# The 16 by 16 diagonal blocks of a delta rule's triangular system, inverted by column elimination on VectorE after a trip through HBM, in place of repeated squaring on TensorE

## The reference, cut to what matters

```
a_kk = where(ii > jj, (kb @ k^T) * decay, 0)     # strictly lower triangular, 64 x 64
m    = a_kk + eye(64)
sol  = triangular_solve(m, [v * beta, kb * exp(gc)], lower, unit diagonal)
```

## Time and profile before

| | |
|---|---|
| median of three runs | 1122.15 us |
| span of the profiled execution, first to last instruction | 1117.9 us |
| the profiled execution's own time | not recorded beside its span; the runs' median lies 4.25 us above this span |
| PE busy | 1053.7 us, 94% |
| DVE, ACT, POOL busy | 279.4, 172.6, 8.5 us |
| read from HBM | 424.29 MB, 382 GB/s over the span |

### The profile page before, as it was taken

How to read it: one execution, slowest core, us unless ns; L and a number is a source line. 1 busy time by engine, 2 the same in 40 slices (tenths; PEclk the granted TensorE clock), 3 DMA queues, 4 the chain that set the end, 5 groups by cost and what they waited for, 6 DMA issues and landing times.

```text
span 1117.9 us, 12901 instructions
## 1 busy us (share of the span) xinstructions
PE 1053.7 (94%) x5140; PEld 448.4 (40%) x5140; DVE 279.4 (25%) x640; ACT 172.6 (15%) x285; POOL 8.5 (1%) x29
## 2 busy tenths in 40 slices
PE   9999999999999999999999888898999898889987
PEld 7866676544343434443333222323333232222322
DVE  3643454432222223331211111111111111111111
ACT  3522344300000000000100000000000000000001
POOL 1000000000000000000000000000000000000000
PEclk9999999999999999999999999999999999999999
DMA  9594137799999999999999999999999999999996
GB/s 325 110 349 180 76 116 293 306 428 399 422 412 425 430 429 429 427 429 430 433 434 429 430 429 431 431 431 429 432 430 428 427 431 433 431 433 424 425 428 281
DMA packets 37931, 427.48 MB, mean 382 GB/s; under 512 B 6243, under 2 KB 8388, under 8 KB 17924
## 3 DMA queue, kind: packets, MB, share of 16 engines
q1 hardware_dynamic: 36628, 426.37, 91.6%
q10 hardware_dynamic: 1264, 0.56, 0.2%
HBM read 424.29 MB, written 2.62 MB: 382 GB/s over the span
## 4 chain that ended last, share of the span: by engine, by line
PE 56%; DMA 37%; DVE 4%; issue 1%; ACT 1%; SPq 0%; DVEq 0%; ACTq 0%
DMA store<-in_w_gate_up_dram 21%; PE bank L1900 18%; DMA store<-in_w_down_dram 15%; PE bank L1950 14%; PE bank L1475 5%; PE bank L1485 4%; PE bank L1676 4%; PE bank L1818 3%; PE bank L1550 2%; PE bank L1880 1%; DVE flow L1329 1%; DMA store<-in_w_in_dram 1%; PE bank L1919 1%; DVE flow L1322 1%; DVE flow L1327 1%
## 5 line engine op out<-in xcount | busy, mean ns | idle before, releaser
L1900 PE MATMUL bank<-store,flow 128*64 128x512 f32 x2048 | 450.9, 596 | 14.0 <-DMA store<-in_w_gate_up_dram 13.1
L1900 PEld LDWEIGHTS bank<-store,flow 128*64 128x64 f32 x2048 | 144.1, 137 | 315.5 <-issue 288.7
L1950 PE MATMUL bank<-store,flow 128*64 128x512 f32 x992 | 230.3, 617 | 33.6 <-DMA store<-in_w_down_dram 21.4
L1322 DVE TENSOR_SCALAR flow<-bank 128x512 f32<-128x512 f32 x32 | 22.1, 692 | 597.4 <-PE bank L1900 597.4
L1950 PEld LDWEIGHTS bank<-store,flow 128*64 128x64 f32 x992 | 74.1, 141 | 169.5 <-issue 143.2
L834 ACT ACTIVATE flow<-flow 128x512 f32<-128x512 f32 x32 | 20.2, 631 | 449.5 <-DVE flow L1322 449.5
L1827 PE MATMUL bank<-qkT 64*128 64x512 f32 x248 | 61.9, 616 | 0.0
L1475 PE MATMUL bank<-store 128*128 128x512 f32 x128 | 57.2, 595 | 0.0
L850 ACT COPY qkT<-bank 128x512 f32<-128x512 f32 x31 | 18.2, 586 | 204.9 <-PE bank L1950 204.9
L1485 PE MATMUL bank<-store 128*128 128x256 f32 x192 | 42.9, 381 | 0.4 <-DMA store<-in_w_in_dram 0.4
L1485 PEld LDWEIGHTS bank<-store 128*128 128x128 f32 x192 | 36.2, 190 | 6.9 <-issue 2.2
(11 more groups left out here) (322 smaller groups left out, 631.4 us busy)
## 6 DMA issues: line engine op xcount, KB each, us to landing
store<-in_w_gate_up_dram SPq DMA_DIRECT2D x38, 4096.0 KB, 26.8
store<-in_w_down_dram SPq DMA_DIRECT2D x60, 2048.0 KB, 18.9
store<-in_w_gate_up_dram SPq DMA_DIRECT2D x51, 2048.0 KB, 14.3
store<-in_w_in_dram SPq DMA_DIRECT2D x6, 2048.0 KB, 21.0
store<-in_w_out_dram SPq DMA_DIRECT2D x1, 4096.0 KB, 18.3
store<-in_w_down_dram SPq DMA_DIRECT2D x3, 1024.0 KB, 30.6
store<-in_w_in_dram SPq DMA_DIRECT2D x2, 1024.0 KB, 9.0
store<-in_w_gate_up_dram SPq DMA_DIRECT2D x2, 1024.0 KB, 7.5
```

Source lines behind the costliest of these rows:

```text
L1900: ins = mm(dst[SLOTS * hf:SLOTS * (hf + 1), :], rows[:, c:c + SLOTS], store[:, slot_at(j, odd) + c0:slot_at(j, odd) + c0 + 512], start=Fal ...
L1950: ins = mm(dst[SLOTS * hf:SLOTS * (hf + 1), :], turned[:, c:c + SLOTS], w[:, hf * 512:(hf + 1) * 512], start=f == 0, stop=f == KT - 1)
```

## The change

Stages 3 to 6 go, and the part of stage 2 that turned N. In their place:

- Each 16 by 16 block has only 16 columns that matter, so after stage 1 DVE sums N over the eight blocks' columns (`reduce_sum`, to 128 by 64 values for each tile).
- When both tiles' sums are there, SyncE writes them to HBM, 1,024 pieces of 64 bytes, waits, and reads them back with one block on each of 64 partitions, 64 pieces of 1 KB.
- A new step J on DVE inverts all 64 blocks at once by columns: a copy, a memset and 28 small operations, each waiting for the one before.
- SyncE writes the inverses to HBM (64 pieces), waits, and reads them back by columns (1,024 pieces of 64 bytes). The expert's tiles are issued behind this on SyncE.
- A new step E on DVE spreads the 16 columns over the 128 and masks them with a block mask that POOL makes at the start; the result is G. Stage 7 then needs 0E or 1E.

The order string is new up to "z14", and the same as before from "s0 O2 S4 18" on. Lines of it at that place, before and now:

```diff
-    text = ("z7 01 11 y8 02 z8 y9 12 z9 y10 13 03 14 z10 04 y11 05 n0 z11 06 f0 f1 15 f2 f3 y12 S0 z12 07 P0 S1 "
-            "y13 z13 P1 08 T0 16 S2 09 O0 P2 17 T1 0A S3 O1 P3 0B y14 T2 0C 0M z14 1K s0 O2 S4 18 ...
+    text = ("z7 01 11 y8 02 z8 y9 12 z9 y10 J0 z10 0E 1E n0 07 y11 17 z11 f0 f1 f2 f3 08 y12 S0 z12 09 P0 S1 "
+            "y13 0A z13 P1 T0 0B S2 O0 P2 T1 0C S3 y14 O1 P3 1K T2 0M z14 s0 O2 S4 18 ...
...
+        n_dram = nc.dram_tensor("fine_blocks", [T * HG, P * FINE], F32, kind="Internal").ap()
+        t_dram = nc.dram_tensor("fine_inverses", [T * HG, P * FINE], F32, kind="Internal").ap()
...
+            def by_column(dram):
+                return bass.AP(dram.tensor, 0, [[FINE, P], [P * FINE, T * HG], [1, FINE]])
+            def by_block(dram):
+                return bass.AP(dram.tensor, 0, [[FINE * FINE, BLOCKS], [1, FINE * FINE]])
+            sp.wait_ge(n_ready, T)
+            sp.dma_start(by_column(n_dram), n_cols).then_inc(st_n, 16)
+            sp.wait_ge(st_n, 16)
+            sp.dma_start(n_sq, by_block(n_dram)).then_inc(ld_n, 16)
+            sp.wait_ge(t_ready, 1)
+            sp.dma_start(by_block(t_dram), t_sq).then_inc(st_t, 16)
+            sp.wait_ge(st_t, 16)
+            sp.dma_start(t_cols, by_column(t_dram)).then_inc(ld_t, 16)
...
+            def invert_blocks():
+                dve.wait_ge(ld_n, 16)
+                st.step(dve.tensor_copy(t_of, n_of.rearrange("q i c -> q c i")))
+                st.step(dve.memset(t_sq[:, 0:FINE * FINE:FINE + 1], 1.0))
+                for j in range(1, FINE - 1):
+                    shape = [BLOCKS, j, FINE - 1 - j]
+                    part = new_of[:, 0:j, j + 1:FINE]
+                    st.step(dve.tensor_tensor(part, n_of[:, j + 1:FINE, j].unsqueeze(1).to_broadcast(shape),
+                                              t_of[:, 0:j, j].unsqueeze(2).to_broadcast(shape), ALU.mult))
+                    ins = dve.tensor_tensor(t_of[:, 0:j, j + 1:FINE], t_of[:, 0:j, j + 1:FINE], part, ALU.add)
+                    ...
...
+                        nr.mark(dve.reduce_sum(n_cols[:, HG * t:HG * (t + 1), :],
+                                               m["N"].rearrange("p (h b j) -> p h j b", h=HG, j=FINE), AX_X))
                     elif s == 2:
-                        st.step(dve.tensor_copy(m["D"], X[:]))
-                        st.step(dve.tensor_tensor(heads(m["G"]), heads(m["D"]), each_head(ident[:]), ALU.add))
                         gdn.mark(dve.tensor_tensor(heads(m["H"]), heads(Z[:]), wide(gd[:, 2, t], P), ALU.mult))
...
+                    elif s == "E":
+                        dve.wait_ge(ld_t, 16)
+                        dve.wait_ge(block_mask, 3)
+                        gdn.mark(dve.tensor_tensor(m["G"] ..., t_cols[...] ..., same_block ..., ALU.mult))
...
                     elif s == 2:
-                        flip(X, m["N"])
                         pe.wait_ge(silu_ready, 6)
                         ins = flip(Z, vt)
-                    elif s == 3:
-                        product(X, m["D"], m["N"])
-                        ins = product(Y, m["N"], m["D"])
-                    elif s == 4:
-                        product(X, m["F"], m["E"])
-                        product(Y, m["E"], m["F"])
-                        ins = product(Z, m["E"], m["G"])
-                    elif s == 5:
-                        product(X, m["D"], m["N"])
-                        ins = product(Z, m["N"], m["G"])
-                    elif s == 6:
-                        ins = product(X, m["E"], m["G"])
```

More of the change, by code:

```diff
@@ L29 @@
 SLOTS = 64
+FINE = 16
+BLOCKS = 64
 MASKED = -1e30
@@ L62, in attention_order @@
 def attention_order():
-    text = ("z7 01 11 y8 02 z8 y9 12 z9 y10 13 03 14 z10 04 y11 05 n0 z11 06 f0 f1 15 f2 f3 y12 S0 z12 07 P0 S1 "
-            "y13 z13 P1 08 T0 16 S2 09 O0 P2 17 T1 0A S3 O1 P3 0B y14 T2 0C 0M z14 1K s0 O2 S4 18 T3 P4 W0 O3 0N "
+    text = ("z7 01 11 y8 02 z8 y9 12 z9 y10 J0 z10 0E 1E n0 07 y11 17 z11 f0 f1 f2 f3 08 y12 S0 z12 09 P0 S1 "
+            "y13 0A z13 P1 T0 0B S2 O0 P2 T1 0C S3 y14 O1 P3 1K T2 0M z14 s0 O2 S4 18 T3 P4 W0 O3 0N "
             "19 T4 0D 1A S5 O4 1B W1 P5 T5 X0 1C O5 1M X1 w0 1N W2 A0 H0 H1 1D R0 L0 W3 G0 M0 X2")
-    names = {str(i): i for i in range(10)} | {"A": 10, "B": 11, "C": 12, "D": 13, "K": "K", "M": "M", "N": "N"}
+    names = {str(i): i for i in range(10)} | {"A": 10, "B": 11, "C": 12, "D": 13} | {c: c for c in "EKMN"}
     return [("gdn", int(w[0]), names[w[1]]) if w[0] in "01" else (w[0], int(w[1:]), None)
@@ L79 @@
 ORDER = attention_order()
[L80 to L83, removed]
+PE_STAGES = {1, 2, 7, "K", 8, 9, 10, 11, 12, 13}
+DVE_STAGES = PE_STAGES | {"E", "M", "N"}
+ACT_STAGES = {7, 8, 9, "M", "N"}
+BANK4_STAGES = {2, 8, 9}
 BANK4 = [step for step in ORDER if (step[0] == "gdn" and step[2] in BANK4_STAGES)
@@ L227, in hybrid_layer @@
         cw_rows = mats[0:CONV_K * 12, 5, 0:P]
+        n_cols = MAT[0]["E"][:, 0:P].rearrange("p (g j) -> p g j", j=FINE)
+        n_sq, t_sq = (MAT[0]["F"][0:BLOCKS, FINE * FINE * i:FINE * FINE * (i + 1)] for i in range(2))
+        t_new = MAT[1]["E"][0:BLOCKS, 0:FINE * FINE]
+        t_cols = MAT[1]["F"][:, 0:P].rearrange("p (g i) -> p g i", i=FINE)
+        same_block = gate[:, 1, 3 * P:4 * P]
         fdist = pt[0:HS, 0, 0:TW]
@@ L312, in hybrid_layer @@
         gdn_psum, gdn_dve, gdn_act = sem("gdn_psum"), sem("gdn_dve"), sem("gdn_act")
+        n_ready, st_n, ld_n, t_ready, st_t, ld_t = (
+            sem(n) for n in ("n_ready", "st_n", "ld_n", "t_ready", "st_t", "ld_t"))
         s_psum, s_max, p_exp, p_ready, pt_psum, pt_ready, o_psum, o_ready = (
@@ L601, in _ @@
                                       channel_multiplier=-1))
+            sb_ = Tally(pool, block_mask)
+            blocks = same_block.rearrange("p (b n) -> p b n", n=FINE)
+            sb_.step(pool.memset(same_block, 1.0))
+            sb_.step(pool.affine_select(blocks, blocks, [[FINE, P // FINE], [0, FINE]], ALU.is_ge, 0.0,
+                                        base=FINE - 1, channel_multiplier=-1))
+            sb_.mark(pool.affine_select(blocks, blocks, [[-FINE, P // FINE], [0, FINE]], ALU.is_ge, 0.0, base=0,
+                                        channel_multiplier=1))
             sq = Tally(pool, swa_sq)
@@ L1063, in shares @@
                 st.step(dve.tensor_scalar(gates[t], share[t], nrm[:, 7, 4 + t:5 + t], None, ALU.mult))
+            nr = Tally(dve, n_ready)
+            n_of, t_of, new_of = (m.rearrange("q (a b) -> q a b", b=FINE) for m in (n_sq, t_sq, t_new))
+            def invert_blocks():
[8 more added lines that the diff above has]
+                    ins = dve.tensor_tensor(t_of[:, 0:j, j + 1:FINE], t_of[:, 0:j, j + 1:FINE], part, ALU.add)
+                    if j < FINE - 2:
+                        st.step(ins)
+                    else:
+                        Tally(dve, t_ready).mark(ins)
             n_exp = 0
@@ L1083, in _ @@
                 if kind in "syfWXLTR":
+                    continue
+                if kind == "J":
+                    invert_blocks()
                     continue
@@ L1625, in _ @@
                     continue
[L1626 removed]
+                if kind in "snwARGPJ":
                     continue
```

19 lines of the change are left out of this document (8 added, 11 removed).

## The result

The changed kernel takes 1125.1 us (median of 6 runs, 1123.2 to 1125.96), the kernel before 1120.7 (6 runs beside it, 1118.89 to 1122.41): a ratio of 1.0038, 95% interval 1.0027 to 1.0048, so slower by 4.3 us (3.0 to 5.4). Forecast were 1126.0 us and slower.

A forecast was written before the change was run, and what follows sets the result against it. TensorE was taken to bound the kernel before the expert loop: -15.2 + 12.6 + 1.7 + 5.2 - 0.4 = +3.9 us, on span 1117.9 plus 4.25, gives 1126.0 us; range 1118.5 to 1131.

The forecast's parts named there:

- What goes, -15.2: On TensorE, 16 removed groups at 0.893 us and two turns of N at 0.435 us save 15.2 us.
- -0.4: Two earlier TensorE waits between 140 and 160 us, 0.44 us idle, are better covered now: 0.4 us saved.
- The first write at 89.7: SyncE's first write of the column sums, held behind queued weights, lands at 89.7 us, 0.8 behind the last piece.
- The three other transfers: Round trip after the first write: read by blocks 2.4 us, write by blocks 2.4, read by columns 3.5 (2.3 fixed plus 1.2).
- J, 7.0 us: On DVE, 28 small operations at 0.23 us, 6.4 us, plus 0.6 for copy and memset; bounds 5.8 to 8.6.
- The stall, 12.6: TensorE stands still from 93.4 to 106.0 us, waiting for 0E ahead of stage 7 of tile 0: +12.6 us.
- The clock, +1.7: After the stall TensorE runs at a granted clock of 0.50: +1.7 us, or 0.6 if 128-column groups hardly feel it.
- The covers, +5.2: Waits exposed on TensorE by removed groups: unit 12 1.6, 09 0.8, "T0" 0.8, "T1" 1.8, "f3" 0.15; +5.2 us (3 to 6.5).
- not held by the queue: Rival: the first write passes the weights, landing by 79 us; stall 1.9, no clock lost, -8.5, so 1113.7 us; chance 0.10.
- Shorter stall: Rival: landings of 2.0 us, J 5.8, half the lost covers; stall 10, clock 1.0, 1120.2 to about 1122 us; chance 0.20.
- Small pieces are slow: Rival: two transfers of 1,024 pieces take 5.3 us each; stall 17, about +8, 1130 us; chance 0.13.
- swallowed: Rival: the expert loop swallows the loss because transfers set the pace there; 1122.2 us; chance 0.05.

The follow-up runs named there:

- moving the load away: Changed kernel with the output projection's weights (4 MB) issued behind the round trip's four transfers on SyncE: 1115.9 us, ratio 0.9965.
- the control in the kernel before: Kernel before, with the output projection's weights loaded behind the last two pieces of the projection's weights, no round trip: 1120.4 us, ratio 0.9997.
- the run with 128 pieces: Changed kernel with first write and its read issued by ScalarE, the write in 128 pieces of 512 bytes: 1119.9 us, ratio 0.9990.
- The other order: Changed kernel with five steps (S0, S1, P1 and 0B, P2 and 0C) in other places in the order string: 1121.1 us, ratio 1.0006.
- the write on an empty queue: Changed kernel with the first write done twice, the second starting on an empty queue: 1127.0 us, ratio 1.0057.

## Why the prediction was right

The mechanism was as forecast, and the sum came out right partly by luck: the stall was forecast 0.9 too long and the clock 1.4 too cheap, and within the stall the transfers were 1.9 too long and J 0.85 too short. Forecast +3.9, measured +3.9 at SyncE's first issue of the expert loop. That the two agree to a tenth is luck as well: TensorE was 0.7 us early in the profiled execution.

- **What goes, -15.2.** Not measured by itself. The kernel without the trip has neither the stall nor the half clock, and issues at 206.13 against 216.06, 9.9 us earlier; by -15.2 + 4.8 - 0.4 it would be 10.8. Of what is missing 0.3 was there before the change acts (unit 9 started at 83.20, and not at 83.80 - 0.87 as from the kernel before). So the three terms together are right to about 0.6 us; which of them the rest belongs to is open. The -0.4 shows by itself: the kernel before waits 0.3 and 0.2 us between 55 and 210, and neither wait is left.
- **TensorE done at 93.4**: it was at 104.36 - 11.66 = 92.7, and between 92.8 and 94.0 in the other runs.
- **The first write at 89.7**: 89.34. The hold is shown by moving the load away (3.9 us from issue to landing) and by the control in the kernel before. The step's reason, the order within the queue, is right for the queue it is on: there the small packets stand behind all the weights. But it would not have been cured by another queue: there the write waits for a turn for each of its 1,024 packets (11.3 us), and with 128 packets it still took 6.65.
- **The three other transfers** took 2.13, 1.98 and 2.25, forecast 2.4, 2.4 and 3.5. The last was the most oversized: small pieces cost next to nothing here, and the 1.2 us for them were taken from a row with other data ahead.
- **J, 7.0 us**: 7.85, and within its bounds. Per operation the forecast was near (0.17 to 0.24 us and small gaps), but one operation of J takes 0.8 to 1.0 us instead of 0.2 in each profile, and not always the same one (at 87.19 above, of 54 elements). The timeline shows beside what:

```profile
93.40 1.04 POOL L647 TENSOR_TENSOR store<-store 128x512 f32<-128x512 f32 x1 [5.83 <-ACT store L696]
93.59 0.91 DVE L1115 TENSOR_TENSOR store<-store 64x44 f32<-64x44 f32 x1
```

GpSimd's operation on a unit of the projection runs from 93.40 to 94.44, and DVE's, which began within it, ends at 94.50. So it is in all eleven profiles with J: the long operation starts 0.1 to 0.6 us behind the start of this one on GpSimd and ends 0.03 to 0.07 us behind its end, wherever the two meet. In the run with 128 pieces two of GpSimd's fell within J, and there J's first copy took 0.77 us instead of 0.37 as well. No run moved GpSimd's operation, so this is read from the places alone: which operation is long follows GpSimd's place in every run. It is 0.6 to 0.8 us of the path that the prediction didn't have.

- **The column sums** took 1.0 us each, not 0.7; the second is done at 75.1, as forecast (75.3), since DVE was earlier with stage 1 in this execution.
- **The stall, 12.6**: 11.66. Its bounds, 9.5 to 17, don't follow from their parts: with three transfers behind the first landing at 2.0 to 5.3 us and J at 5.8 to 8.6 they are 9.1 and 21.8. The 12 us of work that were to hide "n0" are 10.4 by the earlier trace rows (four groups and unit 11); it hid all the same.
- **The clock, +1.7**: 8.31 - 5.22 = 3.1 in the changed kernel. This is the term that was mis-sized most. It was taken from a stall of 2.5 us. The runs give, for stalls of 3.8, 6.6, 8.4, 9.2, 11.3, 11.7 and 13.0 us, a price of 1.7, 2.4, 2.9, 2.1, 2.1, 3.1 and 1.9: more than 1.7 as a rule, and not in step with the stall's length. The run with 128 pieces adds 2.3 us for a stall of 7.8. In each 0.3 us are of the start and not of the clock. After 0.4 and 1.4 us of standstill the granted clock stays at 1.00.
- **The covers, +5.2**: 1.5 + 0.8 + 0.8 + 1.7 = 4.8, each within 0.1 us of its own forecast; "f3" showed no wait. The other order took 3.6 of it back by the medians.
- **From the sum to the time.** The 4.25 us on top of the span were too much: the changed kernel's profiled execution took 1123.86 with a span of 1122.0, so 1.9 lie around it. More of the 4.25 was the scatter of three runs: the kernel before has 1120.7 over six. That is why 1126.0 stands 0.9 above the median while the forecast difference (3.9) is below the measured one (4.3).

Of the rivals, "not held by the queue" (1113.7) is out, though moving the load made nearly that kernel: 1115.9. Its price was too low: with the write landed at 79.4, J still has to wait for stage 2 of tile 1 on DVE, and the stall is 3.8 and not 1.9, with half clock behind it. "Shorter stall" was right on the landings (2.0 us), but J and the covers cost as forecast; by its own parts its stall is 9.1, not 10, and its lower end 1119.3, so the 1118.5 of the stated range isn't worked out from anything. "Small pieces are slow" and "swallowed" are refuted by the write on an empty queue (2.14) and by the kernel without the trip (13.8 less).

## What to carry to other kernels

A trip through HBM costs its four landings, here 2.0 to 2.25 us each however small the pieces, only where the DMA engines are idle. Beside a stream of weights it stands behind them on the same queue and takes a turn per packet on another; so move the loads that nobody needs soon behind it. Where that can't be, another queue with few, long pieces helps in part (6.65 us for the write and 5.3 for the read, against 2.1 each when idle). Count the gap that it leaves on the bounding engine with the half clock behind it (1.7 to 3.1 us here, after 3.8 to 13 us), and look for work that fits into it. When groups are removed from a full engine, look for the waits that they covered: a new order of the steps that remain gave most of them back. And when small operations go to DVE, look what GpSimd runs beside them.

## What was not expected of the hardware

- Two queues share the DMA engines by packets and not by bytes (912 to 913): 64 KB in 1,024 pieces took 11.3 us beside a stream of 2 KB packets, in 128 pieces 6.65, and alone 2.14. Beside the stream the first packets go 3.5 us after the issue, alone 0.9.
- The price of the half clock doesn't grow steadily with the stall between 3.8 and 13 us (1.7 and 1.9 at the ends, 3.1 at 11.7).
- Writing 64 KB as 1,024 pieces of 64 bytes took 2.14 us, as 64 pieces of 1 KB 1.98.
- A DVE operation of 14 to 54 elements that starts while GpSimd's L647 runs ends only with it, having taken 0.6 to 0.8 us more than otherwise, in all eleven profiles.
